# A network of two blocks on one core: seven re-orderings around the waits of its matmul stream

## What is computed

```python
def first_block(...):                       # DEPTH = 2 layers
    for l in range(DEPTH):
        h_l = rmsnorm(x_lat, norm_mix_pre[l]) * (1.0 + sc1_l) + sh1_l      # and h_c for the context
        m_l, m_c = hybrid_mixer(h_l, h_c, ...)    # q,k,v,z,xbc,dt = h @ w_in; attention; conv + SSD scan; @ w_out
        x_lat = x_lat + g1_l * rmsnorm(m_l, norm_mix_post[l])
        f_l = rmsnorm(x_lat, norm_ffn_pre[l]) * (1.0 + sc2_l) + sh2_l
        x_lat = x_lat + g2_l * rmsnorm(swiglu(f_l, w_gate[l], w_up[l], w_down[l]), norm_ffn_post[l])
        # l == 0 only: the same for the context
def ssd_output(y, xs, z, n):
    y = (y + d_skip[:, None] * xs).reshape(b, n, SSD_WIDTH)
    return rmsnorm(y * silu(z), ssd_norm)
def second_block(...):                      # layer 0: sparse attention + SwiGLU
    for layer in range(DEPTH):              # layer 1: native sparse attention + 8 experts (2 per token)
        if layer == 1: kc, vc, k_slc, v_slc, k_win, v_win = nsa_shared_kv(h, ...)
        h = h + a_gate[:, None, :] * mix(modulate(rmsnorm_2(h, attn_gain[layer]), a_shift, a_scale))
        u = modulate(rmsnorm_2(h, ffn_gain[layer]), f_shift, f_scale)
        h = h + f_gate[:, None, :] * (swiglu_2(u, ...) if layer == 0 else moe_swiglu(u, ...))
    return rmsnorm_2(h, final_gain)
```

## Time and profile before

| | |
|---|---|
| median of 3 runs | 2930.82 us (2928.22 to 2939.82) |
| profiled execution | 2934.96 us, its span 2933.7 us |
| PE busy | 2715.8 us, 93% of the span |
| DVE busy | 2000.3 us, 68% |
| ACT busy | 1485.1 us, 51% |
| mean granted clock of PE | 0.95 |
| chain of work that ended last | PE 81%, DVE 10%, ACT 6%, DMA 2% |
| DMA | mean 230 GB/s |

### The profile page before, as it was taken

One profiled execution on the slowest core, in us unless ns is written; L12 is line 12 of the kernel. 1 busy time (PEld: TensorE's weight loads), 2 busy tenths in 40 slices (PEclk: granted clock), 3 DMA queues, 4 the chain that ended last, 5 costly groups with the idle time before them and its releaser, 6 DMA issues.

```text
span 2933.7 us, 33017 instructions
## 1 busy us (share of the span) xinstructions
PE 2715.8 (93%) x13394; PEld 2137.6 (73%) x13394; DVE 2000.3 (68%) x2327; ACT 1485.1 (51%) x1663; POOL 120.9 (4%) x172
## 2 busy tenths in 40 slices
PE   6988889999988978998889989999999999999997
PEld 3766577777766646776767767878888888888886
DVE  4565365446556535447854566689989989999998
ACT  4332264335343234335543344666776766767665
POOL 3023000000000310000000000000000000000000
PEclk8998899999999978999999999889999999999999
DMA  7443445665643464653256443079999999999996
GB/s 261 173 148 101 173 165 187 240 213 203 215 172 145 144 214 145 229 198 123 87 188 231 162 139 130 11 285 365 351 358 357 352 352 359 364 349 359 358 360 230
DMA packets 292877, 674.26 MB, mean 230 GB/s; under 512 B 19462, under 2 KB 115846, under 8 KB 259440
## 3 DMA queue, kind: packets, MB, share of 16 engines
q1 hardware_dynamic: 286368, 662.26, 63.5%
q0 software_dynamic: 4912, 6.67, 0.9%
q10 hardware_dynamic: 1440, 3.16, 0.3%
HBM read 670.93 MB, written 1.10 MB: 229 GB/s over the span
## 4 chain that ended last, share of the span: by engine, by line
PE 81%; DVE 10%; ACT 6%; DMA 2%; issue 1%; SPq 0%; POOL 0%; ACTq 0%; DVEq 0%; POOLq 0%
PE psum L544 22%; PE psum L546 21%; PE psum L545 21%; PE psum L76 8%; PE psum L378 3%; DVE wslot_r L554 2%; PE psum L1443 1%; ACT whi_r L76 1%; PE psum L1961 1%; DVE cacc L76 1%; PE psum L1578 1%; PE psum L2939 1%; DMA first<-in_w_mod 1%; DVE dec L76 1%; DVE x L76 1%
## 5 line engine op out<-in xcount | busy, mean ns | idle before, releaser
L544 PE MATMUL psum<-whi_r,xhi_r 128*128 128x512 f32 (+1 forms) x752 | 303.1, 403 | 12.0 <-DVE xlo_r L554 8.3
L554 DVE TENSOR_TENSOR wslot_r<-wslot,whi_r 128x2048 fp32r<-128x2048 f32 (+1 forms) x114 | 255.7, 2252 | 68.9 <-ACT whi_r L76 66.7
L546 PE MATMUL psum<-whi_r,xlo_r 128*128 128x512 f32 (+1 forms) x752 | 295.0, 392 | 0.0
L545 PE MATMUL psum<-wslot_r,xhi_r 128*128 128x512 f32 (+1 forms) x736 | 289.9, 394 | 0.0
L554 DVE TENSOR_TENSOR wslot_r<-wslot,arena_r 128x2048 fp32r<-128x2048 f32 x113 | 258.5, 2288 | 29.8 <-ACT arena_r L2883 29.6
L554 DVE TENSOR_TENSOR dslot_r<-dslot,wide_r 128x2048 fp32r<-128x2048 f32 x110 | 251.5, 2286 | 28.4 <-ACT wide_r L2897 28.1
L2883 ACT ACTIVATE arena_r<-wslot 128x2048 fp32r<-128x2048 f32 x112 | 215.0, 1919 | 91.5 <-DMA wslot<-in_moe_w_gate 44.9
L2897 ACT ACTIVATE wide_r<-dslot 128x2048 fp32r<-128x2048 f32 x110 | 210.6, 1918 | 96.3 <-DMA dslot<-in_moe_w_down 96.3
L76 ACT ACTIVATE whi_r<-wslot 128x2048 fp32r<-128x2048 f32 (+1 forms) x114 | 212.5, 1875 | 39.8 <-PE psum L76 23.0
L554 DVE TENSOR_TENSOR dslot_r<-dslot,ld_hi_r 128x2048 fp32r<-128x2048 f32 x44 | 100.6, 2292 | 187.5 <-ACT ld_hi_r L76 187.5
L545 PE MATMUL psum<-wslot_r,arena_r 128*128 128x512 f32 x560 | 220.7, 394 | 0.0
(11 more groups left out here) (547 smaller groups left out, 6104.3 us busy)
## 6 DMA issues: line engine op xcount, KB each, us to landing
wslot<-in_moe_w_gate SPq DMA_DIRECT2D x112, 1024.0 KB, 5.0
wslot<-in_moe_w_up SPq DMA_DIRECT2D x112, 1024.0 KB, 5.0
dslot<-in_moe_w_down SPq DMA_DIRECT2D x110, 1024.0 KB, 4.9
dslot<-in_w_mod SPq DMA_DIRECT2D x35, 1024.0 KB, 4.8
wslot<-in_w_gate SPq DMA_DIRECT2D x66, 512.0 KB, 5.5
wslot<-in_w_up SPq DMA_DIRECT2D x66, 512.0 KB, 6.3
dslot<-in_w_down SPq DMA_DIRECT2D x33, 1024.0 KB, 4.9
mod_half<-in_w_ada SPq DMA_DIRECT2D x27, 1024.0 KB, 4.8
```

The source lines that it names most:

```text
L544: t.matmul(out_, hi, w_hi, start=start, stop=False)
L545: t.matmul(out_, hi, w_lo, start=False, stop=False)
L546: return t.matmul(out_, lo, w_hi, start=False, stop=stop)
L554: return v.tensor_tensor(one_pass(lo), src, one_pass(hi), ALU.subtract)
```

## The change

It re-orders work in seven places; what is computed stays the same.

1. `rstd_steps`: the two halves' sums of squares are not added first. DVE makes `lifted` from the first half, ACT's Sqrt takes the second with it as bias, and the refinement has one operation fewer. `squares` returns both marks and can do one half alone.
2. Scan's tail: a yield after the root and one before each tile's scale-and-gain.
3. `joint_out`: the first weight halves are rounded and the first tiles turned at once, a free down slot is fetched ahead; the norm rows are loaded from SP's queue behind a wait on the newest DVE and ACT work; columns and gates are asked for after them. In layer 0 the first context tile is finished behind piece (1, 2) instead of (0, 2). In layer 1 the first half of the second tile's square is taken inside the last piece.
4. `turn_x`, `turn_b` rotate over banks 4 to 6; in layer 1 three of the turn_x move from tile Q_ into tile X1_.
5. `Line.run`: `finish_off(waiting)` straight behind `up(0, 0)`.
6. `Line.run(root_first=True)` for the ffn's Line: the next chain's root is taken two steps earlier.
7. `native_attention`: the second chain is advanced ahead of the first and of the weight split, Q0_ is split whole, and both pieces of Q1_ come ahead of the windows of their tile.

```diff
-    def rstd_steps(dst, m_, n, after, name):
-        ready = ve.op(v.tensor_scalar, m_, dst, 1.0 / n, EPS, ALU.mult, ALU.add, after=after)
-        rooted = ac.put(a.activation, dst, m_, ACT.Sqrt, after=[ready])
+    def rstd_steps(c0, n, squared, name):
+        dst, m_, a_, b_, t_ = (st[:, c:c + 1] for c in (c0, c0 + 1, c0 + 2, c0 + 3, c0 + 4))
+        lifted = ve.op(v.tensor_scalar, t_, a_, 1.0 / n, EPS, ALU.mult, ALU.add, after=[squared[0]])
+        rooted = ac.put(a.activation, dst, b_, ACT.Sqrt, scale=1.0 / n, bias=t_, after=[lifted, squared[1]])
+        ve.op(v.tensor_scalar, m_, b_, 1.0 / n, t_, ALU.mult, ALU.add, after=[squared[1]])
         yield name
         ve.op(v.reciprocal, dst, dst, after=[rooted])
-        ve.op(v.tensor_tensor, m_, m_, dst, ALU.mult)
-        ve.op(v.tensor_tensor, m_, m_, dst, ALU.mult)
-        ve.op(v.tensor_scalar, m_, m_, -0.5, 1.5, ALU.mult, ALU.add)
-        return ve.op(v.tensor_tensor, dst, dst, m_, ALU.mult)
+        ve.op(v.tensor_scalar, t_, dst, dst, m_, ALU.mult, ALU.mult)
+        ve.op(v.tensor_scalar, t_, t_, -0.5, 1.5, ALU.mult, ALU.add)
+        return ve.op(v.tensor_tensor, dst, dst, t_, ALU.mult)
...
                 self.up(n, 0)
+                if n == 0 and waiting:
+                    finish_off(waiting)
...
                 beside(n)
                 if n:
                     modulate(n)
-                if n == 0 and waiting:
-                    finish_off(waiting)
...
-            to(chains[0], "added")
+            to(chains[0], "rooted" if root_first else "added")
             self.up(end, 1)
             fetch_next(1)
             preload(ACT.Silu)
             self.gate(end, 1)
+            if root_first:
+                to(chains[0], "turn")
             self.hidden(end, 1)
-            to(chains[0], "rooted")
+            if not root_first:
+                to(chains[0], "rooted")
...
-            to(chains[0], "turn")
+            to(chains[0], "late" if root_first else "turn")
             self.downs(end, (1,))
...
         def turn_x(t4):
-            s, c0 = t4 // 2, 2 + (t4 % 2) * P
-            bk = bank_for_pe(4)
+            s, c0, b_ = t4 // 2, 2 + (t4 % 2) * P, 4 + t4 % 3
+            bk = bank_for_pe(b_)
...
             elif j == X1_:
                 if p_ == 1:
                     split_tile(Q_)
+                if p_ == 2:
+                    turn_x(0)
+                    turn_x(1)
+                if p_ == 3:
+                    turn_x(2)
                 conv(4 + p_)
             elif j == Q_:
                 if p_ == 2:
                     split_tile(Z_)
-                    turn_x(0)
-                    turn_x(1)
                     norm_k()
                 if p_ == 3:
-                    turn_x(2)
                     turn_x(3)
...
-        rstd_in(few[:, 24 + first:28], few[:, 28 + first:32], 512)
+        root, lifted = few[:, 24 + first:28], few[:, 28 + first:32]
+        ve.op(v.tensor_scalar, lifted, root, 1.0 / 512, EPS, ALU.mult, ALU.add, after=[ac.now()])
+        rooted = ac.put(a.activation, root, lifted, ACT.Sqrt, after=[ve.now()])
+        yield
+        ve.op(v.reciprocal, root, root, after=[rooted])
+        for _ in range(2):
+            ve.op(v.tensor_tensor, lifted, lifted, root, ALU.mult)
+        ve.op(v.tensor_scalar, lifted, lifted, -0.5, 1.5, ALU.mult, ALU.add)
+        ve.op(v.tensor_tensor, root, root, lifted, ALU.mult)
         for t4 in range(first, TB):
+            yield
             y = cat4[:, t4, 512:1024]
...
-        meet4()
-        settle()
-        load_columns(f"mod{l}", (1, 1, 1), (1, 2, 1))
-        ask_gates(f"mod{l}", *((CTX, 2), (LAT, 2), (CTX, 5), (LAT, 5)) if l == 0 else ((LAT, 2), (LAT, 5)))
-        load_rows((prow[:, 0, :], i["norm_mix_post"][l].partition_broadcast(P)),
-                  (prow[:, 1, :], i["norm_ffn_post"][l].partition_broadcast(P)))
...
+        if free_first[0] not in slot_at.values():
+            fetch_part(0)
+        meet4()
...
+        rounded = [high_part(0, half) for half in range(2)]
+        mod_step()
+        low_part(0, 0, rounded[0])
+        settle()
+        turn_cat(first)
+        low_part(0, 1, rounded[1])
+        turn_cat(first + 1)
+        if not parts[1]:
+            fetch_part(0)
+        fetch_part(1)
+        for dst, src in ((prow[:, 0, :], "norm_mix_post"), (prow[:, 1, :], "norm_ffn_post")):
+            sp.wait(ve.now(), ac.now())
+            nc.sync.dma_start(dst, i[src][l].partition_broadcast(P)).then_inc(s_row, 16)
+            rows[0] += 16
+        load_columns(f"mod{l}", (1, 1, 1), (1, 2, 1))
+        ask_gates(f"mod{l}", *((CTX, 2), (LAT, 2), (CTX, 5), (LAT, 5)) if l == 0 else ((LAT, 2), (LAT, 5)))
         if l == 0:
-            split(0, 0)
-            turn_cat(0)
-            split(0, 1)
-            turn_cat(1)
...
-                    if j == 0:
+                    if j == (1 if t4 == 2 else 0):
                         finish_off(chain)
...
-        piece(1, 3, lambda: finish_off(c0))
+        early = []
+        piece(1, 3, lambda: (early.extend(row_squares(1, (0,))), finish_off(c0)))
...
+        to(c1, "added")
+        to(c0, "half")
+        to(c1, "rooted")
         to(c0, "late")
-        to(c0, "half")
-        to(c1, "x")
-        to(c1, "rooted")
+        to(c1, "turn")
         finish_off(c0)
-        b_in.split(Q0_, halves=(0,))
-        to(c1, "turn")
+        b_in.split(Q0_)
         gate_read()
-        b_in.split(Q0_, halves=(1,))
...
         project(Q0_, 1)
+        project(Q1_, 0)
         windows(0)
         twice(256)
         blocks(0)
-        project(Q1_, 0)
+        project(Q1_, 1)
         windows(1)
-        project(Q1_, 1)
         blocks(1)
```

More of the change, by code:

```diff
@@ L720, in onward @@
         yield "added"
+        squared = []
         for h in range(2):
             hs = slice(h * 512, (h + 1) * 512)
-            squared = ac.put(a.activation, temp[:, hs], x[:, s, tt, hs], ACT.Square, accum_out=parts[:, h:h + 1], after=[added[h]])
+            squared.append(ac.put(a.activation, temp[:, hs], x[:, s, tt, hs], ACT.Square, accum_out=parts[:, h:h + 1],
+                                  after=[added[h]]))
         yield "x"
-        summed = ve.put(v.tensor_tensor, ss, parts[:, 0:1], parts[:, 1:2], ALU.add, after=[squared])
-        known = yield from rstd_steps(ss, m_, D, [summed], "rooted")
+        known = yield from rstd_steps(c0, D, squared, "rooted")
         normed = {}
@@ L730, in onward @@
             normed[half] = ac.put(a.activation, temp.rearrange("p (m k) -> p m k", k=KD)[cols],
-                                  x[:, s, tt, :].rearrange("p (m k) -> p m k", k=KD)[cols], ACT.Copy, scale=ss, after=[known, squared])
+                                  x[:, s, tt, :].rearrange("p (m k) -> p m k", k=KD)[cols], ACT.Copy, scale=ss, after=[known, squared[1]])
         yield "turn"
@@ L1136, in turn_x @@
                 turned = pe.free(t.transpose, bk[:, b * P:(b + 1) * P], xbcT[:, b, s, c0:c0 + P], ident[:])
-            read_by(4, ac.put(a.activation, xtok[:, t4, :], bk, ACT.Copy, after=[turned]))
+            read_by(b_, ac.put(a.activation, xtok[:, t4, :], bk, ACT.Copy, after=[turned]))
         def turn_b(s):
-            bk = bank_for_pe(5)
+            b_ = 5 + s
+            bk = bank_for_pe(b_)
             pe.wait(silu_of[5])
@@ L1646, in joint_out, with high_part, low_part @@
             landed[1].append((s.sem, s.n))
[L1647 removed]
+        if free_first[0] not in slot_at.values():
+            fetch_part(0)
+        meet4()
+        his = [whi[u][:].rearrange("p (k n) -> p k n", k=KD) for u in range(2)]
+        slot0, tile0, landed0 = fetched
+        parts[0], landed[0] = [tile0[:, 0:4], tile0[:, 4:8]], landed0
+        w_low, cat_split, done = {}, {}, {}
+        def high_part(j, half):
+            ks = slice(4 * half, 4 * half + 4)
+            return ac.put(a.activation, one_pass(his[j][:, ks]), parts[j][half], ACT.Copy, after=[landed[j][half]])
+        def low_part(j, half, rounded):
+            ks = slice(4 * half, 4 * half + 4)
+            w_low[j, half] = ve.put(low, parts[j][half], parts[j][half], his[j][:, ks], after=[rounded])
         def split(j, half):
[L1650 to L1652 removed]
+            low_part(j, half, high_part(j, half))
         def turn_cat(t4):
@@ L1686, in own_banks, with row_squares, from_banks @@
             return psum[:, 2 * tt:2 * tt + 2, :].rearrange("p b n -> p (b n)")
-        def from_banks(s, tt, gain, sets, ready_, t0=0):
+        def row_squares(tt, which):
+            t4 = 2 + tt if l else tt
+            return squares(tt, lambda h: psum[:, 2 * tt + h, :], lambda h: spare[:, tt, h * 512:(h + 1) * 512],
+                           [done.get((h, t4)) for h in range(2)], which)
+        def from_banks(s, tt, gain, sets, ready_, t0=0, early=()):
             t4 = 2 + tt if l else tt
             marks = (done[0, t4], done[1, t4])
```

(13 more changed lines are left out.)

32 lines of the change are left out of this document (14 added, 18 removed).

## The result

The changed kernel takes 2892.62 us in the median of its first four runs (2879.19 to 2904.1), the kernel before 2929.52; the ratio is 0.9863 with a 95% interval of 0.9829 to 0.9896. Run again beside seven runs of the kernel before, it took 2890.76 against 2933.99, ratio 0.9845 (0.9822 to 0.9868). The forecast was 2886 with a range of 2868 to 2908, a gain of 45: the measured gains are 37 and 43.

A forecast was written before the change was run, and what follows sets the result against it. Ahead of the experts' stage the prediction took PE's stream to be bound by waits, each costing idle time and half-clock work behind it. Terms summed to 47.4 us; 45 was taken, giving 2886 us, range 2868 to 2908.

The forecast's parts named there:

- Scan's tail: Scan's tail in both layers: shorter PE waits for PTj and less half-clock work behind them, 8.1 and 6.2 us gained.
- joint_out, layer 0: Layer 0's joint_out: 5.4 us from earlier weights at its start, 4.0 from turning the first tile behind the third piece.
- joint_out, layer 1: Layer 1's joint_out: late norm rows move PE's wait to the second piece instead of removing it, 1.5 us lost.
- Turned banks, layer 1: Layer 1's joint_in: rotated banks and early turn_x remove the 10.92 wait, then VectorE's chain decides; 5.5 us gained.
- Layer 0: The same turned banks in layer 0: two thirds of the 2.1 us of other xtok waits, 1.4 us gained.
- Line: Line in layer 1 and the ffn: finishing the second tile earlier shortens waits of 9.54 and 8.40; 6.5 and 4.6 gained.
- Shorter root chains: Root chains lose two small VectorE operations each, which shows only where PE waits for the chain; 1.2 us gained.
- Ffn's tail and native attention: Ffn's tail and native_attention: waits of 4.46 and 5.22 fall to 3.6 each, that of 3.29 goes; 6.0 us gained.
- The clock that isn't given back: Rival: remaining and new waits still drop PE's clock, so the gain is 30 and the time 2901; chance 0.20.
- the experts' stage is untouched: Last 1000 us of the kernel: the change edits nothing there, so the stage can only start earlier.
- The column loads: Rival: 1 MB modulation column loads bound the mixes, the two scans' 14.3 is lost, time 2901; chance 0.08.
- SP's wait: Rival in both joint_outs: loads queued behind SP's wait land late and PE idles, 49 us more, 2935; chance 0.03.

The follow-up runs named there:

- u_jout: The changed kernel with the whole function joint_out of before, shorter root kept; 2889.35 us.
- f_gain: The changed kernel with row_gain in layer 1's joint_out moved behind the two splits of the second column half; 2884.27 us.
- u_turns: The changed kernel with turn_x and turn_b as before: banks 4 and 5 only, all four turn_x of layer 1 in tile Q_; 2887.84 us.
- u_move: The changed kernel with rotated banks kept but turn_x(0) to (2) of layer 1 back in tile Q_; 2886.37 us.
- u_line: The changed kernel with Line's second tile finished after the side work again, as before; 2897.3 us, ratio 0.9915 to the kernel before.
- u_root: The changed kernel with the first tile's root behind Line's last products again in the ffn's tail, native_attention's new order kept; 2883.13 us.
- a0_after: The changed kernel unedited, run again; 2890.76 us against 2933.99 for the kernel before, ratio 0.9845.

## Why the prediction held, step by step

**The sum.** 47.4 was worked out against the profiled execution. The two profiled executions of the changed kernel are 40.8 and 46.5 shorter, and the means of all runs differ by 43.6. The 45 that was taken holds. The split into idle time (33) and clock (14) is met by the second trace (33 and 14) and by the estimate over all runs (31 and 12), not by the first trace (37 and 4).

Part of the closeness is luck. The parts as measured below, each by its stage, add up to 49, 5 more than the whole. The native attention's second part, which no term of the forecast counts, took 3.3 longer in both traces of the changed kernel than in that of before.

**Scan's tail: 14.3 worked out, 13.0 as the mean of many traces.** The idle time is as worked out in layer 0 (4.0, measured 4.0) and near it in layer 1 (2.9, measured 3.3). The clock's part fits in layer 1 (3.3, measured 3.8). In layer 0 it is too large (4.1, measured 1.9): all of the half-clock work in that stretch was counted as gained, and in five of twelve executions it is still there.

**joint_out, layer 0: 9.4 worked out, 9.1 measured** as the mean of 8.2 and 8.7 against u_jout and 9.5 and 10.0 against before. The new wait at Line's first product was put at 1.0 and is 1.17.

**joint_out, layer 1: a loss of 1.5 worked out, 2.4 to 2.8 measured.** The mechanism was right: the wait moved in front of the second piece. Counted from cat4's turn, that piece starts at 16.4 us where 17.7 was worked out, since the rows landed in 5.8 us and not 7.9. The step that was off is the piece itself: it was priced at full clock (5.1 us to its end), but behind the moved wait of 7.13 its first matmuls run at the lower clock (0.80 for the first) and it takes 7.6. The sum had priced half-clock work behind the waits that go, and none behind the one that comes. That the weights behind the rows were the next thing late was not foreseen; f_gain showed it.

**Turned banks, layer 1: 5.5 worked out, 5.8 by u_turns.** Right that VectorE's key and query chain decides in the end; wrong to count on the early turns for it: u_move has the gain without them, to within 1 us. **Layer 0: 1.4 worked out, 2.9 by the mean.** In the first trace only 1.2 of it shows and in the second 3.6. The longer wait for the modulation's columns (4.17) is in both, and the idle time fell by 2.6 and 1.4, so what differs is the clock.

**Line: 6.5 and 4.6 worked out, 6.8 and 5.2 measured**, with the idle time left (4.2 and 4.4) at 4.30 and 4.29. The make-up is not as worked out: up to 1.4 was put on the early square and the shorter root, but by u_line and u_jout the place of the step took away the whole 5.2 of idle time in layer 1.

**Shorter root chains: 1.2 worked out, not measured by itself.** No run undoes them. The wait of 1.63 that they were to shorten is 0.94 and 1.10 in the two traces.

**Ffn's tail and native attention: 6.0 worked out, 9.9 against the changed kernel's two traces and 8.7 by the means.** The three waits are as worked out (3.44 for 3.6; 3.41 for 3.6; the third gone), and so is their idle time (5.8, measured 6). So the term that was mis-sized is the clock, put at 0.2 and otherwise left to the high end; by the means it is some 2.5. It isn't fixed by the waits: behind the same wait of 3.44 some traces run at full clock and others don't (last section). u_root adds that the early root and the order behind it can't be priced apart.

**The rivals.** The clock that isn't given back: largely true in the first trace (3.7 of 14 came back), untrue in the second (13.7) and by the estimate over all runs. That the experts' stage is untouched held: from its first gather product to the span's end 1011.9 before, 1012.2 and 1012.6 after. The column loads didn't become the bound: the idle time in both mixes fell by what the scan's waits gave. SP's wait did cost something, as the earlier trace rows let one expect, but 2.6 us and not 49: they had landed when VectorE's row gain began at 1074.89, while the second piece was next. The Trainium skill's page "TensorE: Matmul & The Clock Gate", section "HAM oscillation — how this bites in real kernels", says that compute cut by waits starts cold each time. Behind the remaining waits of 7.13 and 4.30 PE does start at the lower clock (0.80 and 0.79 for the first matmul), and behind the one of 3.41 too (0.80). Behind that of 3.44 it starts at 0.50 in both traces of the changed kernel. So the rule holds here for the long ones and not each time behind the shorter ones.

## What to carry to other kernels

In a stream on one engine, price a removed wait twice, by its idle time and by the slow work behind it, but take the second from several traces. Check an edit in the stage that it touches; here the medians of four runs put an edit of 6 us at zero and one of 1 us at 6.5. When a load is moved behind a wait, follow the loads queued behind it as well: the second of them was the next bound.

## What the runs showed of the hardware

The same kernel, run again, gets its full clock at other places. In the native attention's second part the length took only a few values in fourteen traces, 91.6 to 91.7, 94.9 to 96.5, 98.9 and 102.1 to 102.2, whatever had been edited elsewhere; in the changed kernel 131 matmuls ran at 0.51 over 28 us in which PE was busy for 27.3. So a half-clock stretch can go on while PE hardly pauses. The whole time of a run moves by about 2 us for each 0.001 of the mean granted clock (29 runs of the kernel before: 2922.9 at 0.956, 2946.02 at 0.945). What decides the place of such a stretch was not tried and stays open.

The length of a wait alone doesn't decide what stands behind it either. In ten traces PE waits 3.44 us in front of the native attention's first product. The matmul behind it took 0.50 in five of them (the changed kernel's two among them) and 0.79 or 0.80 in the other five, as in u_move:

```profile
1658.61 0.80 PE L544 MATMUL psum<-early_r,xh_q_r 128*128 128x512 f32 x1 [3.44 <-DVE xl_q_r L554]
```

Behind the waits of 4.28 to 4.30 in Line and of 7.1 in joint_out it took 0.79 or 0.80 in every trace that has them. Where PE runs faster, part of the gain can return as idle time: a0_after has 10.0 us less of busy time and 4.3 more of idle time than the first trace of the same kernel.
